# Attention of a two-layer trunk: weighted sums of two turns in one instruction, and other homes for the output weights

## The reference

```
scores = q @ k.T * 64**-0.5, masked
probs  = softmax(scores)               # layer 0: with a sink term in the sum
out    = probs @ v                     # per query block, over its key blocks
mix    = out @ w_out                   # 1024 x 1024, both layers
```

## Time and profile before

| | |
|---|---|
| median of 3 runs | 1077.22 us (1074.67 to 1078.15) |
| the profiled execution | 1075.44 us, span 1073.6 us |
| PE busy | 1056.8 us, 98% |
| DVE, ACT, POOL busy | 748.7, 538.6, 189.3 us |
| attention of layer 0 (slots 1 to 17) | from about 55 to 153 us |
| attention of layer 1 (slots 1 to 17) | from about 607 to 715 us |

### The profile page before, as it was taken

How to read it: one execution, slowest core, us unless ns; L and a number is a source line. 1 busy time by engine, 2 the same in 40 slices (tenths; PEclk the granted TensorE clock), 3 DMA queues, 4 the chain that set the end, 5 groups by cost and what they waited for, 6 DMA issues and landing times.

```text
span 1073.6 us, 14865 instructions
## 1 busy us (share of the span) xinstructions
PE 1056.8 (98%) x5408; PEld 859.5 (80%) x5408; DVE 748.7 (70%) x1286; ACT 538.6 (50%) x1016; POOL 189.3 (18%) x333
## 2 busy tenths in 40 slices
PE   9999999999999999999999999999999999999997
PEld 8877779888888888888778766679888888888886
DVE  5455636596697696687589898526596696696685
ACT  6677645253453453425554567745254443453422
POOL 0464320000000000005413387520000000000005
PEclk9999999999999999999999999999999999999999
DMA  9531505544535445422613333006553535535402
GB/s 301 115 79 41 118 1 133 123 100 97 115 82 118 105 92 118 96 62 53 140 36 79 79 79 80 1 1 144 112 111 86 118 79 118 115 82 118 106 12 79
DMA packets 52009, 99.94 MB, mean 93 GB/s; under 512 B 4704, under 2 KB 4832, under 8 KB 51936
## 3 DMA queue, kind: packets, MB, share of 16 engines
q1 hardware_dynamic: 51216, 98.61, 40.4%
q10 hardware_dynamic: 720, 0.38, 0.1%
HBM read 96.88 MB, written 2.10 MB: 92 GB/s over the span
## 4 chain that ended last, share of the span: by engine, by line
PE 91%; DVE 5%; issue 1%; ACT 1%; DMA 1%; POOL 0%; DVEq 0%; POOLq 0%; SPq 0%; ACTq 0%
PE bank L2062 11%; PE bank L2060 11%; PE bank L2061 11%; PE bank L2437 7%; PE bank L2435 7%; PE bank L2436 7%; PE bank L2070 6%; PE bank L2072 6%; PE bank L2071 6%; PE bank L2219 3%; PE bank L2461 2%; PE bank L2460 2%; PE bank L2459 2%; PE bank L2288 2%; PE bank L2274 2%
## 5 line engine op out<-in xcount | busy, mean ns | idle before, releaser
L2060 PE MATMUL bank<-r_hi,w_hi 128*128 128x512 f32 (+1 forms) x456 | 177.5, 389 | 0.0
L2061 PE MATMUL bank<-r_hi,w_lo 128*128 128x512 f32 (+1 forms) x456 | 177.4, 389 | 0.0
L2062 PE MATMUL bank<-r_lo,w_hi 128*128 128x512 f32 (+1 forms) x456 | 177.4, 389 | 0.0
L1651 DVE TENSOR_TENSOR w_lo<-w_raw,w_hi 128x1024 fp32r<-128x1024 f32 x84 | 102.0, 1222 | 70.9 <-ACT w_hi L1170 70.7
L1170 ACT ACTIVATE w_hi<-w_raw 128x1024 fp32r<-128x1024 f32 x84 | 88.0, 1056 | 119.4 <-PE bank L2062 82.9
L2435 PE MATMUL bank<-w_hi,hid_hi 128*128 128x512 f32 x336 | 130.7, 389 | 0.0
L2436 PE MATMUL bank<-w_lo,hid_hi 128*128 128x512 f32 x336 | 130.7, 389 | 0.0
L2437 PE MATMUL bank<-w_hi,hid_lo 128*128 128x512 f32 x336 | 130.7, 389 | 0.0
L1179 ACT ACTIVATE w_hi<-w_raw,gT 128x512 fp32r<-128x512 f32 x96 | 64.5, 716 | 106.6 <-DMA w_raw<-in_w_mlp_up 75.1
L814 POOL TENSOR_TENSOR acc<-acc,G 128x512 f32<-128x512 f32 x8 | 13.0, 1651 | 594.3 <-ACT waste L1026 594.3
L2062 PEld LDWEIGHTS bank<-r_lo,w_hi 128*128 128x128 f32 (+1 forms) x456 | 85.2, 187 | 18.2
(11 more groups left out here) (215 smaller groups left out, 2149.4 us busy)
## 6 DMA issues: line engine op xcount, KB each, us to landing
w_raw<-in_w_mlp_up SPq DMA_DIRECT2D x64, 512.0 KB, 6.4
w_raw<-in_w_mlp_down SPq DMA_DIRECT2D x64, 512.0 KB, 6.9
w_raw<-in_b_w_in SPq DMA_DIRECT2D x16, 512.0 KB, 6.8
w_raw<-in_a_w_in SPq DMA_DIRECT2D x8, 512.0 KB, 9.3
w_raw<-in_a_w_out SPq DMA_DIRECT2D x8, 512.0 KB, 5.8
w_raw<-in_b_w_out SPq DMA_DIRECT2D x8, 512.0 KB, 6.0
xt<-in_x_turned SPq DMA_DIRECT2D x8, 256.0 KB, 4.9
X<-in_x SPq DMA_DIRECT2D x4, 512.0 KB, 11.1
```

What stands on the lines that cost most here:

```text
L1651: nc.vector.tensor_tensor(half_of(w_lo[:, u % 2, :], a), b_of(PRODUCTS[i][1], a), half_of(w_hi[:, u % 2, :], a).bitcast(f32), ALU.subtract ...
L2060: nc.tensor.matmul(bank, whi, xhi, start=start, stop=False)
L2061: nc.tensor.matmul(bank, wlo, xhi, start=False, stop=False)
L2062: return nc.tensor.matmul(bank, whi, xlo, start=False, stop=stop)
```

## The change

The weighted sums of a pair's two turns are made together, in odd slots only: in slot 2m+3 for pair m (turns 2m, 2m+1), with one matmul of 512 columns for each key block and key head, where there were two of 256. Its moving operand takes the copies of both turns, which lie in two of the eight places of `pt`; a table gives each copy its place and the sum that must be done before it. Even slots have no weighted sums.

The second output unit of a layer (7, 61) gets its home in the first half of the memory of the normed input, which is free when the first rows' half of the input projection is done; the third (8, 62) gets a working place. Units 7 and 8 are split one slot earlier (7 in slot 8, 8 in slot 9, 9 in slot 10), unit 61 two slots earlier (slot 3), 62 one (slot 5). Unit 61 is no longer shared: ACT makes all of its high part, POOL all of its low part.

```diff
+PV_AT = [0]
+for _l in range(DEPTH):
+    for _m in range(TURNS // 2):
+        PV_AT.append(PV_AT[-1] + len(key_blocks(_l, PAIRS[_l][_m][1])))
+LATE_PAIRS = {4: ((0, 5), (1, 6), (2, 7)), 5: ((3, 5), (4, 6), (1, 7)), 6: ((0, 1), (2, 5), (3, 6), (4, 7)),
+              7: ((0, 1), (2, 5), (3, 6), (4, 7))}
+def pt_places(layer, m, c):
+    if layer and m in LATE_PAIRS:
+        return LATE_PAIRS[m][c]
+    return 4 * (m % 2) + c, 4 * (m % 2) + 2 + c
+def pt_uses():
+    places, freed, holder = [], [], {}
+    for layer in range(DEPTH):
+        for n in range(TURNS):
+            m, rh = divmod(n, 2)
+            for c in range(len(key_blocks(layer, turn(layer, n)[1]))):
+                place = pt_places(layer, m, c)[rh]
+                places.append(place)
+                freed.append(holder.get(place, 0))
+                holder[place] = PV_AT[8 * layer + m] + c + 1
+    return places, freed
...
-SPLITS = ({-1: (4,), 1: (5,), 6: (6,), 8: (7,), 9: (8,), 10: (9,)}, {1: (60,), 4: (61,), 5: (62,), 6: (63,)})
-NEXT_SLOT = (5, 6, 7, 8, 9, 61)
+SPLITS = ({-1: (4,), 1: (5,), 6: (6,), 7: (7,), 8: (8,), 9: (9,)}, {1: (60,), 2: (61,), 4: (62,), 6: (63,)})
+NEXT_SLOT = (5, 6, 7, 8, 9)
-SHARED = 61
...
-            if name[:3] == "out" and n >= 2:
-                ks = slice(4 * n - 8, 4 * n - 4)
+            if name[:3] == "out" and n % 2:
+                ks = slice(2 * n - 2, 2 * n + 2)
...
-            s = 1 if name == "ki" else u % 2
+            s = 1 if name == "ki" or name[:3] == "out" and n else u % 2
...
-            if name[:3] == "out" and n >= 2:
-                return U[name] - 1
+            if name[:3] == "out" and n:
+                return U[name] - 2 if n == 1 else U[name] - 1
             if name[:3] == "mlp" and n in (2, 3):
-                return u - 6
+                return U["out1" if u >= U["qi"] else "out0"] + 2 * (n - 2)
...
-            def shared_split():
...
-                        if u == SHARED:
-                            shared_split()
-                        elif u in POOL_UNITS:
+                        if u in POOL_UNITS:
                             split_low(u, (0, 1))
...
-                if K >= PT_PLACES:
-                    act.wait_ge(pv_done, K - PT_PLACES + 1)
-                nc.scalar.activation(pt[:, K % PT_PLACES, :], banks[t_bank(layer, ("pt", K))][:], ACT.Copy).then_inc(pt_out, 1)
+                if PT_FREED[K]:
+                    act.wait_ge(pv_done, PT_FREED[K])
+                nc.scalar.activation(pt[:, PT_PLACE[K], :], banks[t_bank(layer, ("pt", K))][:], ACT.Copy).then_inc(pt_out, 1)
...
-            def weighted(layer, n, c):
+            def weighted(layer, m, c):
...
                 for a in range(2):
                     g = 2 * p + a
-                    ins = nc.tensor.matmul(bank[64 * a:64 * a + 64, 256 * rh:256 * rh + 256],
-                                           kvs[:, kbs[c], KVD + HD * g:KVD + HD * g + HD], pt[:, K % PT_PLACES, 256 * a:256 * a + 256],
-                                           start=c == 0, stop=c == len(kbs) - 1)
+                    ins = nc.tensor.matmul(bank[64 * a:64 * a + 64, :], kvs[:, kbs[c], KVD + HD * g:KVD + HD * g + HD],
+                                           pt[:, low:high + 1:high - low, 256 * a:256 * a + 256], start=c == 0, stop=c == len(kbs) - 1)
...
-                    summing = len(pt_of(layer, n - 2)) if n >= 2 else 0
+                    pair = (n - 3) // 2 if n >= 3 and n % 2 else None
+                    summing = 0 if pair is None else len(key_blocks(layer, PAIRS[layer][pair][1]))
...
-                        weighted(layer, n - 2, c)
+                        weighted(layer, pair, c)
```

More of the change, by code:

```diff
@@ L144, in pt_of @@
     return range(PT_AT[16 * layer + n], PT_AT[16 * layer + n + 1])
+PV_AT = [0]
[19 more added lines that the diff above has]
+    return places, freed
+PT_PLACE, PT_FREED = pt_uses()
 FILL_IN = (12, 20)
@@ L908, in _ @@
                     for u in SPLITS[layer].get(n - 2, ()):
-                        if u in POOL_UNITS and u != SHARED:
+                        if u in POOL_UNITS:
                             split_low(u, (2, 3))
                     for u in SPLITS[layer].get(n - 1, ()):
-                        if u == SHARED:
-                            shared_split()
-                        elif u in POOL_UNITS:
+                        if u in POOL_UNITS:
                             split_low(u, (0, 1))
@@ L955, in split_half @@
                 last = nc.scalar.activation(w_place(u)[0][:, cs], raw(RAW[u][0])[:, cs], ACT.Copy)
-                if part or u == SHARED:
+                if part:
                     last.then_inc(w_hi_done, 1)
@@ L1078, in pt_copy @@
                 act.wait_ge(pt_ready, K + 1)
-                if K >= PT_PLACES:
-                    act.wait_ge(pv_done, K - PT_PLACES + 1)
-                nc.scalar.activation(pt[:, K % PT_PLACES, :], banks[t_bank(layer, ("pt", K))][:], ACT.Copy).then_inc(pt_out, 1)
+                if PT_FREED[K]:
+                    act.wait_ge(pv_done, PT_FREED[K])
+                nc.scalar.activation(pt[:, PT_PLACE[K], :], banks[t_bank(layer, ("pt", K))][:], ACT.Copy).then_inc(pt_out, 1)
             def o_high(layer, pair):
                 p, i = PAIRS[layer][pair]
-                act.wait_ge(pv_done, PT_AT[16 * layer + 2 * pair + 2])
+                act.wait_ge(pv_done, PV_AT[8 * layer + pair + 1])
                 nc.scalar.activation(q_reg(layer)[0][:, 4 * p:4 * p + 4, blk(i)], banks[o_bank(layer, pair)][:].rearrange(
@@ L1112, in attention @@
                     for u in SPLITS[layer].get(n - 1, ()) if n > 0 else ():
-                        if u in HALVED and u != SHARED:
+                        if u in HALVED:
                             split_half(u, 1)
@@ L1701, in t3_sum @@
                 else:
-                    dve.wait_ge(pv_done, PT_AT[16 * (layer + 1)])
+                    dve.wait_ge(pv_done, PV_AT[8 * (layer + 1)])
                 for a in range(2):
@@ L2275, in transposes @@
                 ins.then_inc(pt_ready, 1)
-            def weighted(layer, n, c):
-                N = 16 * layer + n
-                p, i, rh = turn(layer, n)
+            def weighted(layer, m, c):
+                p, i = PAIRS[layer][m]
                 kbs = key_blocks(layer, i)
[L2281 to L2285, removed]
+                pe.wait_ge(pt_out, PT_AT[16 * layer + 2 * m + 1] + c + 1)
+                if c == 0 and m >= 2:
+                    pe.wait_ge(o_lo_done, 8 * layer + m - 1)
+                bank = banks[o_bank(layer, m)]
+                low, high = pt_places(layer, m, c)
                 for a in range(2):
                     g = 2 * p + a
-                    ins = nc.tensor.matmul(bank[64 * a:64 * a + 64, 256 * rh:256 * rh + 256],
-                                           kvs[:, kbs[c], KVD + HD * g:KVD + HD * g + HD], pt[:, K % PT_PLACES, 256 * a:256 * a + 256],
-                                           start=c == 0, stop=c == len(kbs) - 1)
+                    ins = nc.tensor.matmul(bank[64 * a:64 * a + 64, :], kvs[:, kbs[c], KVD + HD * g:KVD + HD * g + HD],
+                                           pt[:, low:high + 1:high - low, 256 * a:256 * a + 256], start=c == 0, stop=c == len(kbs) - 1)
                 ins.then_inc(pv_done, 1)
```

5 lines of the change are left out of this document (1 added, 4 removed).

## The result

The changed kernel takes 1083.33 us (median of 4 runs, 1081.17 to 1084.41), the kernel before in the same comparison 1076.35: a ratio of 1.0066, 95% interval 1.0053 to 1.0079, so 7.0 us slower. The forecast was 1079.5, the range ended at 1083.0. The profiled execution took 1084.41 us, its span is 1082.6.

What follows compares the result with a forecast made beforehand. PE was taken to bound the kernel (busy 1056.8 of 1073.6 us). Layer 0's +2.3 and layer 1's 0.0, with 3.1 gross saving against 5.4 of new waits, put the median 1077.22 at 1079.5 us; range 1074.0 to 1083.0.

Steps and rivals of the forecast that it cites:

- Part 1: Weighted groups on PE: 0.155 us per group plus 0.86 per 512-column key block; 20 fewer groups, gross saving 3.1 us.
- Rival D: Weighted sums: the saving is smaller, up to all but gone, 2.2 us more, 1081.7; chance 0.08.
- Part 2: Order in layer 0: -0.46 up to slot 7, then new waits and moved sums; +2.3 us in all.
- The shift carries the other engines along: Layer 0, slots 2 to 7: PE has no wait to lose cover from, so the change there is -0.46 us.
- Unit 9's data at 109.0: Layer 0: transfer issued at 102.5 lands 6.5 us later, so scores of turn 12 start 1.8 us later.
- Rival C: Layer 0: unit 9's data come later than 109.0, each us going straight into slot 11; one more gives 1080.6; chance 0.12.
- rival B: Layer 1: the clock falls once more, after 3 us of standing before 633.6; costs 1.5 us, 1081.0; chance 0.17.
- Later slots: Layer 0 from slot 11: +0.4 us of moved sums, and +0.55 in slot 16 waiting for ACT's copies.
- Part 3: Order in layer 1: delays from POOL's whole unit 61, moved sums and lost waits sum to 0.0 us.
- POOL's row for turn 5: Layer 1: with unit 61 whole on POOL, turn 5's probabilities end at 633.5.
- the wait of 1.09: Layer 1, slot 8: PE's wait before 650.89, from unit 63's late data, was to go as unit 61 finishes earlier.
- Rivals A and E: Queues don't lengthen or waits are covered, 1072.6, chance 0.14; layer 0 as forecast but layer 1 loses its waits, 1078.0, 0.07.

Runs made afterwards that it cites:

- f1: The changed kernel with PE multiplying the identity in three waits (slot 11 of layer 0, slots 3 and 6 of layer 1): 1081.67 us, ratio 1.0051.
- e1: The kernel before with the 512-column sums alone, homes and units' order as before: 1080.20 us, ratio 1.0037.
- e4: The changed kernel with layer 1's output units as before (61 shared by the engines): 1082.07 us, ratio 1.0059.
- i1: The kernel before with 512-column sums only for the late pairs (5 to 7 in layer 0, 3 to 7 in layer 1): 1078.88 us, ratio 1.0020.
- j1: The late-pairs kernel i1 plus filling matmuls before layer 0's first output step and, in layer 1, in slot 3 and before the first output step: 1078.98 us.
- j2: The kernel before with the homes and order alone, plus filling matmuls in slots 10, 11 of layer 0 and 3, 6 of layer 1: 1078.58 us.
- g1: The changed kernel with unit 7's low part on DVE as four 512-column instructions instead of one of 2048: 1083.37 us, ratio 1.0065.
- h1: The changed kernel with unit 10's transfer held until unit 9 has landed: 1082.90 us, ratio 1.0060.
- f2: The kernel before with filling matmuls in slot 3 and before the first output step of layer 1: 1076.10 us, ratio 1.0003.
- f3: The kernel before with the 512-column sums alone, plus filling matmuls before each layer's first output step and in slot 3 of layer 1: 1078.87 us.
- j3: j1 with 6 more filling matmuls in slot 8 of layer 1: 1077.66 us, ratio 1.0018.

## Why the prediction missed, point by point

**Part 1 was right.** A group of two key blocks with 512 columns starts at 79.63 and the next work at 81.50, 1.87 as forecast; with one block 1.01, with four 3.59 (720.97 to 724.56), all on 0.155 + 0.86 for each block. 136 records went. A pair of two key blocks saves 2 x 1.01 - 1.87 = 0.15, as the cost per group says. Rival D is out. One count was off: the last weighted work of layer 1, the group of 24 records, holds three of the groups that the prediction counted. So there are 38 groups before and 19 after, and the gross saving is 19 x 0.155 = 2.9, not 3.1. The Trainium skill's price ("TensorE: Matmul & The Clock Gate", Back-to-back issue gap) would have the eight records fewer of such a pair save 0.02; the trace does not agree.

**Part 2 failed in three steps, and a fourth came near.** Places are in us from turn 0's transposes.

- "The shift carries the other engines along": not in slot 4, where the query transposes wait 0.72 for POOL's rotation. The sum of 1.01 that left this slot had covered that. So slot 8 starts at 38.73 and not 38.00: 0.73 missed.
- Unit 9's data at 109.0: it came at 55.24, forecast 53.17. Of this 2.07, 0.73 is the item above and 1.25 the transfer (7.75 against 6.5: the end of the traffic was taken for the landing, 0.9, and 0.35 is unit 10's share of the DMA engines). From the data to the scores of turn 12 it is 6.13, forecast 6.1. Rival C came true, with a price of 1.25 where it had 1.
- The clock: the sum had no term for it, and rival B put one more fall in layer 1 alone. It came in slot 11 of layer 0 as well, where nothing behind it absorbs it. The group of eight records that took 1.87 at 79.63 took 3.50 there (119.13 to 122.63), 1.63 more.
- Later slots: +0.4 and +0.55 forecast, 1.08 measured, with the 0.54 in slot 16 where it was put.

Sum: 2.3 forecast, 6.13 measured; 0.73 + 1.25 + 1.63 make 3.61 of the 3.83 between them. POOL's 4.37 and its wait of 0.98 were not foreseen either, but by the rows they lie ahead of longer waits that don't depend on them.

**Part 3 was right up to slot 7.** POOL's row for turn 5 ends at 640.95, in the times of before 633.4, forecast 633.5; slot 7 is 1.3 late, forecast 1.1; the wait of 1.09 went. The fall behind 641.10 (rival B) costs 0.3: f1, without falls, has 109.18 against 109.52. What was missed is in slots 10 to 12: waits of 0.37 for `o_low`, 0.39 for masks and 0.42 for the queries' low part, where I had taken 0.3 for all. That the shorter even slots uncover them is my reading. 0.0 forecast, 1.47 measured. Rivals A and E are out: where a wait went, others came.

**The form of the error.** The sum was built as if each rival came alone. Here C, the fall of B and the small waits came together, and all on one side. And moving a turn's sum from an even slot to the odd one behind it takes cover from whatever wait lies between (slot 4's queries, the first output step in both layers, unit 63's data). The prediction counted this in slots 8 and 10 of layer 0 and missed it in slot 4 and in layer 1. It never asked what the sums cost without the homes: its own terms for layer 0, +0.4 from slot 11 on and +0.55 in slot 16, with nothing saved ahead of the first output step, already make them a loss of about 1 there. e1's expectation overlooked that.

Measured without falls, the sums alone cost 2.7, of which 0.3 is the filling, so against a gross saving of 2.9 they lose 5.3 to 5.6 to such waits. Of the 7.0, about 2.4 is the sums, 2.6 the homes and order, and about 2 the falls of the clock: 1.9 in slot 11 of layer 0 (after against e4, the same program there) and 0.3 in layer 1 (after against f1). After less f1, 6.98 - 5.52 = 1.5, is too low for them by the 0.7 that f1's filling costs. That the fall comes in one execution and not in another is why no single profiled execution gives these parts.

Open stays why i1's and j1's medians are the size they are. In the one profiled execution of j1 a fall follows the wait in slot 8, and filling that wait took 1.2 off the median. Of the other runs only the mean granted clock is known. In j1 the time goes with it: four runs at 0.999 took 1077.11 to 1078.01, six at 0.998 took 1078.57 to 1080.34, one at 0.996 took 1079.55. That fits a fall in about half of its runs but doesn't show it, since j2's profiled execution has 0.998 without a fall. i1's runs don't sort that way (1079.60 at 0.998, 1076.93 at 0.995), so their spread has another cause as well, and that one isn't known.

## What to carry to other kernels

Work that is merged into a later place isn't only saved, it is moved: list every wait that lies between its old place and its new one, for there it was cover, and behind the wait it counts in full. A saving on the busy engine ahead of a wait that another engine ends is worth nothing, and the longer wait can bring a fall of the clock behind it. Take the time of a transfer from its landing, not from the end of its traffic. Where several rivals push the same way and don't exclude each other, the range has to hold their sum.

## What the runs showed of the hardware

- DVE and POOL took turns while DVE subtracted two operands that lie in on-chip memory (`w_raw` and `r_hi`, `w_raw` and `w_hi`): a rotation step of POOL that takes 0.32 took 2.37 beside it, and with the subtraction in four pieces both were slowed (2.50 to 3.81; POOL's four multiplies 3.23 between 2.33 and 4.37). Beside DVE's masks, whose operand is a bank, POOL ran at its 2.33 (98.18, masks at 98.07 and 98.48). The Trainium skill has this ("Advanced Engine Details and Errata", GPSIMD Details): POOL shares an interface with DVE, and conflicts with DVE's instructions of two memory inputs. The trace agrees.
- The same layer 0 program stood 2.02 us and lost its clock in one execution, stood 1.85 and kept it in another; e1 lost it behind 1.85. Each fall is 3.4 us at 0.50, or twice that (g1, h1). The five kernels with PE kept busy in every wait of over 1.5 us (f1, f2, f3, j2, j3) have no fall in the stages of their profiled executions. f3 and j2 have ten of eleven and ten of ten runs within 1.4 us, but f1's runs span 2.3 us and f2's 4.1, so the falls are not all of the scatter.
- A unit's landing, as the waiting engine sees it, came 0.9 to 1.0 us after the last traffic of its transfer (before: 112.9 against 112.0; h1: 110.85 against 109.9).
